# Loading x first, constants through ScalarE's queue, and the first norm made from PSUM

## The reference

```python
def rmsnorm(x, g):
    xf = x.astype(jnp.float32)
    y = xf * lax.rsqrt(jnp.mean(xf * xf, axis=-1, keepdims=True) + RMS_EPS)
    return (y * g.astype(jnp.float32)).astype(x.dtype)

def swiglu_ffn(x, norm_g, w_gu, w_down):
    h = rmsnorm(x, norm_g) @ w_gu
    a, b = jnp.split(h, 2, axis=-1)
    return (jax.nn.silu(a) * b) @ w_down

for layer in range(DEPTH):
    x = x + 0.5 * swiglu_ffn(x, ffn1_norm[layer], ffn1_w_gu[layer], ffn1_w_down[layer])
    xn = rmsnorm(x, mix_norm[layer])
    ...                                  # retention or sparse attention, x = x + m
    x = x + 0.5 * swiglu_ffn(x, ffn2_norm[layer], ffn2_w_gu[layer], ffn2_w_down[layer])
```

## Time and profile before

| what | value |
|---|---|
| time, median of 3 runs | 2365.38 us (2361.45 to 2367.03) |
| span of the profiled execution | 2360.2 us |
| device time of the profiled execution | not given apart; the median of the runs is 5.2 us above the span |
| TensorE busy | 2286.3 us, 97% of the span |
| GpSimd, VectorE, ScalarE busy | 45%, 44%, 36% |
| stretches with TensorE starved at the start | before 33.5 us |

### The profile page before, as it was taken

One profiled execution on the slowest core, in us unless ns is written; L12 is line 12 of the kernel. 1 busy time (PEld: TensorE's weight loads), 2 busy tenths in 40 slices (PEclk: granted clock), 3 DMA queues, 4 the chain that ended last, 5 costly groups with the idle time before them and its releaser, 6 DMA issues.

```text
span 2360.2 us, 30137 instructions
## 1 busy us (share of the span) xinstructions
PE 2286.3 (97%) x10390; PEld 1856.6 (79%) x10390; DVE 1043.0 (44%) x1767; ACT 840.6 (36%) x1267; POOL 1064.1 (45%) x699
## 2 busy tenths in 40 slices
PE   8999999999999899999999999998888889999999
PEld 6888887888888688888788888876677767888887
DVE  5434204566664744330244340078868863443301
ACT  5333213222122433331343331243367764333311
POOL 5444445444444544444454444464145455444442
PEclk9999999999999999999999999999988889999999
DMA  4222223222222132222232222132100012322221
GB/s 156 98 97 93 94 98 112 84 89 71 89 80 90 54 106 98 98 92 95 80 107 96 93 96 98 71 131 90 44 20 19 18 46 72 111 94 98 98 94 57
DMA packets 57780, 202.20 MB, mean 86 GB/s; under 512 B 6859, under 2 KB 7243, under 8 KB 57596
## 3 DMA queue, kind: packets, MB, share of 16 engines
q1 hardware_dynamic: 57724, 201.46, 24.8%
HBM read 199.29 MB, written 2.14 MB: 85 GB/s over the span
## 4 chain that ended last, share of the span: by engine, by line
PE 82%; DVE 10%; issue 4%; ACT 2%; POOL 1%; DMA 0%; DVEq 0%; SPq 0%; ACTq 0%; POOLq 0%
PE ps L711 17%; PE ps L713 17%; PE ps L712 17%; PE ps L739 7%; PE ps L741 7%; PE ps L740 7%; DVE xl L1091 2%; PE ps L729 2%; PE ps L731 2%; PE ps L730 2%; DVE std L1303 1%; PE ps L968 1%; PE ps L953 1%; DVE x L1102 1%; DVE kh L1314 1%
## 5 line engine op out<-in xcount | busy, mean ns | idle before, releaser
L366 POOL TENSOR_TENSOR wl<-raw,wh 128x1024 fp32r<-128x1024 f32 x364 | 879.3, 2418 | 1070.6 <-ACT wh L473 1070.6
L473 ACT ACTIVATE wh<-raw 128x1024 fp32r<-128x1024 f32 x364 | 385.4, 1062 | 1288.2 <-PE ps L713 808.0
L711 PE MATMUL ps<-xh,wh 128*128 128x512 f32 x1792 | 707.6, 395 | 12.8 <-DVE xl L1091 11.4
L712 PE MATMUL ps<-xl,wh 128*128 128x512 f32 x1792 | 698.5, 390 | 0.0
L713 PE MATMUL ps<-xh,wl 128*128 128x512 f32 x1792 | 698.5, 390 | 0.0
L711 PEld LDWEIGHTS ps<-xh,wh 128*128 128x128 f32 x1792 | 337.0, 188 | 98.8 <-DVE xl L1091 15.5
L712 PEld LDWEIGHTS ps<-xl,wh 128*128 128x128 f32 x1792 | 337.1, 188 | 71.1 <-issue 2.9
L713 PEld LDWEIGHTS ps<-xh,wl 128*128 128x128 f32 x1792 | 337.0, 188 | 70.9
L739 PE MATMUL ps<-uh,wh 128*128 (+1 forms) x672 | 266.4, 396 | 0.0
L740 PE MATMUL ps<-ul,wh 128*128 (+1 forms) x672 | 266.4, 396 | 0.0
L741 PE MATMUL ps<-uh,wl 128*128 (+1 forms) x672 | 266.4, 396 | 0.0
(11 more groups left out here) (229 smaller groups left out, 2788.9 us busy)
## 6 DMA issues: line engine op xcount, KB each, us to landing
raw<-stream SPq DMA_DIRECT2D x364, 512.0 KB, 3.2
tn<-rel_rows SPq DMA_DIRECT2D x16, 256.0 KB, 3.2
xin<-x_in SPq DMA_DIRECT2D x4, 512.0 KB, 5.4
out<-xin SPq DMA_DIRECT2D x8, 256.0 KB, 2.5
dec<-c_dec SPq DMA_DIRECT2D x1, 1024.0 KB, 5.5
rotq<-c_rot SPq DMA_DIRECT2D x1, 512.0 KB, 3.1
vf<-gate_w SPq DMA_DIRECT2D x1, 192.0 KB, 2.1
csq<-c_sq SPq DMA_DIRECT2D x1, 128.5 KB, 2.0
```

Of the source, the lines that this page charges most:

```text
L366: nc.gpsimd.tensor_tensor(wl[:, slot, :], raw[:, slot, :], wh[:, slot, :].bitcast(F32), ALU.subtract).then_inc(chunk_lo, 1)
L473: nc.scalar.activation(wh[:, slot, :], raw[:, slot, :], ACT.Copy).then_inc(chunk_hi, 1)
L711: mm(o, w_h, hi, start=k == 0, stop=False)
L712: mm(o, w_h, lo, start=False, stop=False)
```

## The change

Five loads of constants go from SyncE's queue to the head of ScalarE's stream, so that SyncE begins with x. For the first norm alone, ScalarE makes `xh` out of the transposed tile in PSUM instead of out of `x`; VectorE waits for `xh`, then copies the tile to `x`, then makes `xl` out of PSUM too; ScalarE waits for the copy before it squares `x`.

```diff
-            sp.dma_start(relw[0:BUCKETS, :], rel).then_inc(rel_in, 16)
-            sp.dma_start(onehot[:, :], c_rel).then_inc(rel_in, 16)
-            sp.dma_start(csq[:, :], c_sq).then_inc(csq_in, 16)
             for t in range(TT):
                 sp.dma_start(xin[:, t, :], x_in[t * P:(t + 1) * P, :]).then_inc(x_in_landed[t], 16)
-            sp.dma_start(gain[:, :, :], norm_g).then_inc(consts_in, 16)
-            sp.dma_start(qkg[:, :], qk_gain).then_inc(consts_in, 16)
...
+            def norm_first(tiles):
+
+                for d in tiles:
+                    act.wait_ge(x_turned, d + 1)
+                    nc.scalar.activation(xh[:, d, :], ps[:, d, :], ACT.Copy, scale=gain[:, 0, d:d + 1]).then_inc(xh_ready, 1)
+                    act.wait_ge(x_ready, d + 1)
+                    square(0, d)
...
+            act.dma_start(relw[0:BUCKETS, :], rel).then_inc(rel_in, 16)
+            act.dma_start(onehot[:, :], c_rel).then_inc(rel_in, 16)
+            act.dma_start(csq[:, :], c_sq).then_inc(csq_in, 16)
+            act.dma_start(gain[:, :, :], norm_g).then_inc(consts_in, 16)
+            act.dma_start(qkg[:, :], qk_gain).then_inc(consts_in, 16)
             act.wait_ge(consts_set, 3)
...
                 high(chunk(c), first=True)
-                norm_later(0, ([0], [1], [2, 3], [4, 5, 6, 7])[c])
+                norm_first(([0], [1], [2, 3], [4, 5, 6, 7])[c])
...
             for d in range(KT):
-                dve.wait_ge(x_turned, d + 1)
+                dve.wait_ge(xh_ready, d + 1)
                 V.tensor_copy(x[:, d, :], ps[:, d, :]).then_inc(x_ready, 1)
+                V.scalar_tensor_tensor(xl[:, d, :], ps[:, d, :], gain[:, 0, d:d + 1], xh[:, d, :].bitcast(F32),
+                                       ALU.mult, ALU.subtract).then_inc(xn_ready, 1)
                 dve.wait_ge(x_ready, d + 1)
                 if d in (1, 3):
+                    dve.wait_ge(xn_ready, d + 1)
                     V.memset(mark[:, 0:1], 0.0).then_inc(pair_free, 1)
-                if d:
-                    gained_low(0, d - 1)
-            gained_low(0, KT - 1)
```

## The result

The changed kernel takes 2366.96 us as the median of 20 runs (2364.17 to 2370.12), the kernel before 2363.98 us (2361.31 to 2367.03, 20 runs). The ratio is 1.0013, 95% interval 1.0007 to 1.0019: slower by 3.0 us, and less than 0.2%. The forecast had 2366.8 us, a loss of 1.4 us over the three runs then shown, and "within 0.2%" at 0.83. The time lies in the range; the loss is about double the one that was worked out. That the time was hit within 0.2 us is luck: the three runs stood 1.4 us above the median of the 20, and this made up for the 1.6 us that the forecast loss lacked.

The account below looks back on a forecast made before the run. The start of TensorE's norm matmul was taken to bound the kernel. Tile 2's square 0.8 us earlier and 2.2 us more from there gave +1.4 us on 2365.4: 2366.8 us, range 2362 to 2371.

Parts of the forecast that it names:

- One for one: An earlier or later start of the norm's matmul on TensorE goes through to the kernel's end unchanged in size.
- N: Start of the norm's matmul on TensorE (line 749): 33.48 us before, forecast 34.9 us.
- S to N: From the start of tile 2's square on ScalarE to the norm's matmul: 10.87 us before, forecast 13.1, loss 2.2.
- H to S: From the start of ScalarE's first `high` to tile 2's square: forecast starts 10.45 and 21.8 us.
- X: Start of ScalarE's first `xh`: 12.72 us before, forecast 11.9, bounds 11.2 to 12.7; tile 2's square 9.9 us later.
- The first rival: Early chunk and freed port win: landing -1.3, three `low` -0.9, first addition -0.4; -2.6 us, 2362.8; 12%.
- the second rival: Constants land behind x: `onehot` at 9.3 us instead of 3.39, norm's matmul at 40.0; +6.5 us, 2371.9; 8%.
- if `onehot` is microseconds late: Sign of being wrong: the constant for the bias product comes microseconds late, where 0.7 us was assumed.
- The first chunk: First weight chunk lands at 10.35 us instead of 11.65, 1.3 earlier (bounds 0 to 2.5); ScalarE's first `high` starts at 10.45.
- if anything behind 60 us changes its length: Sign of being wrong: work later than 60 us, which the change does not touch, takes a different time.
- TensorE's clock: Rival: clock stays low (1.2 of 2.4 GHz) through tile 7, 2.56 us per k-tile; +4.1 us, 2369.5; 10%.
- it does not do what it says: Rival: the first weight chunk lands no earlier, first `xh` at 12.7 us; +2.2 us, 2367.6; 5%.

Follow-up runs that it names:

- `xl` alone: The kernel before with one edit: VectorE makes the first norm's `xl` from the PSUM tile instead of from `x`; 2361.93 us against 2364.96, ratio 0.9989.

## Why the prediction was right, and where its size was off

**That the moment to follow is the norm's matmul: right.** Behind it the windows from 60 to 2300 us hold the same work (2180.9 and 2181.6 us of TensorE). "One for one" is right only within the noise behind N, which is larger than the loss.

**S to N, +2.2 us: right.** Foreseen 13.1, measured 13.22 and, in two other kernels with that norm, 13.23. The wait on each copy is in the trace (0.8 us a tile), and the norm without it had S to N 3.0 us shorter (13.23 to 10.27).

**H to S from the norm alone: right in its two opposed parts.** From the first `xh` to S I had X + 9.9 and measured 9.87. The relief of GpSimd (-1.4 us, from `xl` alone) and the new waits (+1.3) cancel, so that 10.80 stands against 10.85. The rule that the prediction took from the Trainium skill (SBUF — State Buffer, section Who interferes with whom) agrees with these runs: with at most one SBUF input in `xl`, both engines' long cases are gone, in `xl` alone too, where they still overlap. The first rival's terms for GpSimd, -0.9 and -0.4 us, are the 1.4 us that `xl` alone gives ahead of S. That its whole price, -2.6 us, is near the -2.4 of that kernel is chance: the rival counted an earlier landing (-1.3) and nothing behind S, where 1.0 us came. In the change the waits eat both.

**The constants: the term that was mis-sized.** The prediction said of `onehot`: "I take 0.7 us", and let its mark hold the seventh transpose. Measured: `onehot` 1.7 us late (5.12 against 3.39), and the identity, to which the prediction gave no delay at all, landed at 8.1 us and held the first transpose. So X was 13.16 and not 11.9 us, beyond the bound of 12.7. This is the second rival's mechanism, constants held up by what loads beside them, at a quarter of its price: `onehot` was 1.7 us late where the rival had 5.9, and X 1.3 us later than forecast where the rival had 5.1. The prediction's own sign of being wrong, "if `onehot` is microseconds late", came in part. What it set against this rival, that the engines take turns between the queues, did not keep the constants from being late. The identity put back ahead of x, X was 11.97 and N 35.04, against the forecast's 11.9 and 34.9.

**The first chunk: nearly right.** H was foreseen at 10.45 and came at 10.91, its last releaser being `qkg`, a constant, and not the chunk. So the chunk had landed by then, and how much earlier this profile does not show.

**The sum.** N came at 36.25 instead of 34.9 us. The forecast was 1.35 us too early: 1.26 are X, so the constants, and 0.1 is S to N. Against before, the profiles say +2.8 us. But the profile of before had its first chunk early (11.76 us where that order has 12.26 in the mean); against the mean the loss is 12.26 + 10.85 + 10.87 = 33.98 to 36.25, or +2.3 us. The median of +3.0 (1.7 to 4.5 by the interval) takes in both. The remaining 1.9 us between the two spans (4.7) lie behind N, in work that the change does not touch: 0.8 us up to the end of layer 0 and 1.1 in the sparse attention. The sign "if anything behind 60 us changes its length" is thus below what one profile can tell, and the median of +3.0 us is not accounted for to the last half microsecond.

**TensorE's clock and "it does not do what it says": did not come.** In the changed kernel the granted clock was 0.52 from 19.5 to 22.7 us, ahead of S, and 1.00 from there on, though the k-tiles waited for `xl`; each k-tile took 1.5 us, not 2.56. The queue change alone shows the lower clock behind S, for 0.24 us.

## What to carry to other kernels

Reading a tile from PSUM instead of from its copy in SBUF was worth 2.4 us here, and much of it through another engine: it freed GpSimd. With ScalarE's `xh` out of PSUM too, and VectorE's copy behind it, ScalarE waited for VectorE in seven of eight turns and the kernel was 4.7 us slower than with `xl` alone. So look at which engine in the ring of waits gets a new one before taking the read. A load put on another queue was not free of the first queue's traffic: beside a large transfer the last three constants arrived 1.3 to 1.4 us apart, 6.3 to 8.1 us after their issue, while two of them, issued ahead of x, took 1.9 and 2.7 us. So in this kernel what the first instruction needs goes out ahead of the large transfer, on whichever queue. And where a change acts on 30 us of 2360, compare the pieces of that stretch between traces, the landing that does not repeat apart from the rest.

## What I had not expected of the hardware

Small transfers of 24 KB and 2 KB on ScalarE's queue took 7.2 and 8.1 us to land beside 4 MB on SyncE's, and 2.0 and 1.9 us where SyncE had just begun to issue or had not. On SyncE's own queue, behind x, they took 5.9 and 6.0 us before. The three last constants arrived 1.3 to 1.4 us apart, whatever their size. How the engines share out their turns is not settled by these runs.

The noise of this kernel is not spread evenly. The landing of the first chunk moved by 1.2 us between five kernels with one order of loads. From N to the end the eleven kernels take 2326.1 to 2330.9 us. Of these 4.8 us the sparse attention has the most: from the last residual addition of layer 1's first feed-forward to the first one behind the attention, the eleven take 436.7 to 440.0 us. The rows of the two extremes (ns min/median/max, then first and last start), `xl` from PSUM and the identity back on SyncE's queue:

```profile
L1102 DVE SCALAR_TENSOR_TENSOR x<-ps,x x8: 676/678/692, 1529.2 to 1541.9; 128x512 f32<-128x512 f32 x8
...
L1102 DVE SCALAR_TENSOR_TENSOR x<-ps,x x16: 677/692/693, 1978.6 to 2349.9; 128x512 f32<-128x512 f32 x16
```

```profile
L1110 DVE SCALAR_TENSOR_TENSOR x<-ps,x x8: 676/678/691, 1533.1 to 1545.7; 128x512 f32<-128x512 f32 x8
...
L1110 DVE SCALAR_TENSOR_TENSOR x<-ps,x x16: 676/691/692, 1985.7 to 2357.1; 128x512 f32<-128x512 f32 x16
```

The granted clock of the window from 1600 to 1950 us is 0.90 and 0.89 in these two, and 0.88 to 0.90 in all. Whether the clock makes this spread was not tried.
